# A hybrid decoder layer: its first norm and tail products tile by tile, norm rows loaded early, bias rows late

## What is computed

```
h = rmsnorm(x, norm_mix)
proj = h @ w_in
gate_a, gate_b, z, xbc, dt_raw, c_q, c_kv, kr_raw = jnp.split(proj, SPLIT_POINTS, axis=-1)
ya = ssd_branch(z, xbc, dt_raw, h0, conv_prev, ...)      # causal convolution, chunked scan
yb = mla_branch(c_q, c_kv, kr_raw, ...)                  # latent attention, paged cache
x = x + (sigmoid(gate_a + b) * ya + sigmoid(gate_b + b) * yb) @ w_out
x = x + peer(rmsnorm(x, norm_ffn), ...)                  # 128 gathered experts for each token
```

## Times and profile before

| | us |
|---|---|
| median of 3 runs | 2399.7 |
| lowest and highest of them | 2396.74, 2403.63 |
| the profiled execution, its own time | 2396.4 |
| its span, first to last instruction | 2394.9 |
| PE busy in it | 1992.9 |
| DVE busy | 1516.4 |
| POOL busy | 637.4 |
| ACT busy | 450.7 |

### The profile page before, as it was taken

How to read it: one execution, slowest core, us unless ns; L and a number is a source line. 1 busy time by engine, 2 the same in 40 slices (tenths; PEclk the granted TensorE clock), 3 DMA queues, 4 the chain that set the end, 5 groups by cost and what they waited for, 6 DMA issues and landing times. The chain is left out here.

```text
span 2394.9 us, 26956 instructions
## 1 busy us (share of the span) xinstructions
PE 1992.9 (83%) x9206; PEld 1147.1 (48%) x9206; DVE 1516.4 (63%) x3836; ACT 450.7 (19%) x1358; POOL 637.4 (27%) x592
## 2 busy tenths in 40 slices
PE   6999888898888877777779997878898888777775
PEld 4887655754444422222258875557444443222221
DVE  2464433378777788888524444334787878887874
ACT  1234211121211111111122342101211111111111
POOL 0000000034443444444200000000344434444441
PEclk9999899899999999999979998999999999999998
DMA  5447387399999999999744473873999999999996
GB/s 163 124 142 235 118 294 263 110 375 410 412 416 386 398 388 420 420 420 419 307 150 145 129 250 125 287 254 114 401 414 415 414 386 420 389 420 420 420 418 247
DMA packets 206117, 744.54 MB, mean 311 GB/s; under 512 B 16339, under 2 KB 96651, under 8 KB 137857
## 3 DMA queue, kind: packets, MB, share of 16 engines
q0 software_dynamic: 83008, 581.14, 59.5%
q1 hardware_dynamic: 122960, 161.59, 20.8%
HBM read 731.40 MB, written 11.46 MB: 310 GB/s over the span
## 5 line engine op out<-in xcount | busy, mean ns | idle before, releaser
L1045 PE MATMUL ps<-arena 128*128 128x512 f32 (+1 forms) x2112 | 1012.7, 613 | 234.6 <-DVE arena L1615 234.4
L2117 POOL DMA_INDIRECT arena<-in_peer_uv,arena x528 | 603.4, 1143 | 912.7 <-PE ps L1045 746.6
L1606 DVE CUSTOM_DVE_ANT_0 arena<-arena,h 128x1024 f32<-128x1024 f32 x512 | 627.3, 1225 | 229.1 <-DMA arena<-in_peer_uv,arena 221.6
L1045 PEld LDWEIGHTS ps<-arena 128*128 128x128 f32 (+1 forms) x2112 | 367.8, 188 | 839.3 <-DVE arena L1615 517.8
L484 PE MATMUL ps<-ht_tok,wring 128*128 128x264 f32 (+2 forms) x1728 | 386.3, 380 | 22.8 <-DMA wring<-in_peer_wq 17.1
L484 PEld LDWEIGHTS ps<-ht_tok,wring 128*128 128x128 f32 x1728 | 315.8, 193 | 93.5 <-DMA wring<-in_peer_wq 20.4
L1916 ACT ACTIVATE arena<-arena 128x1 f32<-128x1 f32 x528 | 104.8, 202 | 1027.9 <-DVE arena L1606 1026.6
L1615 DVE TENSOR_SCALAR arena<-consts,arena 128x128 f32<-128x128 f32 (+1 forms) x528 | 181.0, 343 | 30.7 <-ACT arena L1916 30.6
L484 PE MATMUL ps<-arena,wring 128*128 128x264 f32 (+2 forms) x512 | 96.3, 346 | 13.0 <-DMA wring<-in_w_mla_proj 13.0
L484 PEld LDWEIGHTS ps<-arena,wring 128*128 128x128 f32 x512 | 80.9, 200 | 22.9 <-DMA wring<-in_w_mla_proj 13.6
L2101 POOL DMA_DIRECT2D nrow<-in_norm_ffn x2 | 1.1, 534 | 337.8 <-PE ps L802 337.8
(11 more groups left out here) (316 smaller groups left out, 1780.1 us busy)
## 6 DMA issues: line engine op xcount, KB each, us to landing
arena<-in_pages SPq DMA_DIRECT2D x256, 272.0 KB, 4.0
wring<-in_w_in SPq DMA_DIRECT2D x38, 1024.0 KB, 5.7
wring<-in_peer_wq SPq DMA_DIRECT2D x18, 1024.0 KB, 26.1
arena<-in_peer_uv,arena POOLq DMA_INDIRECT x528
h<-in_state_ssm POOLq DMA_DIRECT2D x16, 512.0 KB, 5.3
out<-h POOLq DMA_DIRECT2D x16, 512.0 KB, 4.7
wring<-in_w_ssm_proj SPq DMA_DIRECT2D x8, 1024.0 KB, 8.4
arena<-in_w_out SPq DMA_DIRECT2D x8, 1024.0 KB, 13.2
```

The lines of the kernel that those rows point to most:

```text
L1045: last = pe.matmul(ps[0:outs, SUM_BANK[t] + half, :], diag[:, n % DIAGS, 0:outs], ring[:, HOME[n % RING], D_MODEL + half * 512:D_MODEL + ( ...
L1606: dve.tensor_tensor_reduce(ring[:, HOME[k], 0:D_MODEL], ring[:, HOME[k], 0:D_MODEL], tokens, 1.0, 0.0, ALU.mult, ALU.add, dots[:, column(n ...
L2117: pool.indirect_dma_start(ring[:, HOME[k], :], None, table, bass.IndirectOffsetOnAxis(ap=idx[:, TOPK * u + j:TOPK * u + j + 1], axis=0)).t ...
```

## The change

The reference's arithmetic stays as it is; the order of it and of the loads changes.

- **Norm by tile.** ACT squares tile 0 and takes its root, then squares tiles 1 and 2 and takes both roots. DVE writes `h` tile by tile, with a signal after each. A root of a constant now stands ahead of the squares on ACT.
- **Transposes by tile.** PE turns tile 0 (eight transposes into two banks), then tile 1, then does the first tail product for tile 0, then turns tile 2 (eight small transposes into one bank), then does the tail products of tiles 1 and 2. DVE copies a bank of four chunks at once.
- **Vector rows behind.** The transposes of `vrows` and `cstate` come behind the tail products, and their loads behind weight blocks 0 and 1. ACT's wait for `vt_ready` moves behind the tail.
- **The norm row.** `norm_mix` of both layers and `norm_final` become one tensor `norms`. Row 0 is loaded in the first block. The row of the next layer (or of the final norm) is loaded by POOL in the retrieval, ahead of slot 32. The loads at the start of a layer and of the last block are gone.
- **`wkb` and `wvb`** move on POOL's queue from its start to behind the three states.

```diff
@@ first block, SP
+                sp.dma_start(nrow[:, :], a["norms"][0, :].partition_broadcast(P)).then_inc(sem("first_loads"), 16)
                 sp.wait_ge(sem("x_zeroed"), 1)
@@ PE
+                    def turned_rows(t):
+                        rows = TILES[t][1]
+                        pe.wait_ge(sem("h_ready"), t + 1)
+                        each = 4 if t < 2 else DC
+                        for first in range(0, DC, each):
+                            b = aux.fill()
+                            for c in range(first, first + each):
+                                at = (c - first) * rows
+                                last = turn(ps[:, b, at:at + rows], h[0:rows, t, :].rearrange("p (q c) -> p c q", c=DC)[:, c, :], rows)
+                            aux.filled(last)
+                        marks["ht", t] = aux.n
+                    def first_tail(t):
+                        t0, rows = TILES[t]
+                        pe.wait_ge(sem("aux_free"), 4 + marks["ht", t])
+                        b = wide.fill()
+                        wide.filled(product(ps[0:rows, b, 0:TAIL[0][1]], lambda c: ht[:, c, t0:t0 + rows], lambda c: state["w"][:, c, :], DC))
+                    turned_rows(0)
+                    turned_rows(1)
+                    state["w"] = next_block(DC, TAIL[0][1])
+                    first_tail(0)
+                    turned_rows(2)
+                    marks["ht"] = aux.n
+                    first_tail(1)
+                    first_tail(2)
+                    marks["tail0"] = wide.n
                     pe.wait_ge(sem("vec_loads"), 64)
...
-                    pe.wait_ge(sem("h_ready"), 1)
-                    feature_major(lambda t: h[:, t, :])
-                    marks["ht"] = aux.n
-                    aux.all_emptied()
-                    by_token(*TAIL[0])
-                    marks["tail0"] = wide.n
@@ DVE
+                    rstd(ss[:, 0:1], ss[:, 0:1], rt[:, 0:1], rs[:, 0:1], D_MODEL, "x0_squares", "x0_root")
+                    normed(0)
+                    rstd(ss[:, 1:3], ss[:, 1:3], rt[:, 1:3], rs[:, 1:3], D_MODEL, "x1_squares", "x1_root")
+                    normed(1)
+                    turned_rows(0)
+                    normed(2)
+                    turned_rows(1)
+                    turned_rows(2)
@@ ACT
-                    for t in range(3):
-                        squares(h[:, t, :], x[:, t, :], ss[:, t:t + 1], "x_squares" if t == 2 else None)
-                    root(rt, ss, "x")
-                    act.wait_ge(sem("vt_ready"), 1)
+                    act.activation(st[:, 61:62], ones[:, 0:1], ACT.Sqrt)
+                    squares(h[:, 0, :], x[:, 0, :], ss[:, 0:1], "x0_squares")
+                    root(rt[:, 0:1], ss[:, 0:1], "x0")
+                    squares(h[:, 1, :], x[:, 1, :], ss[:, 1:2])
+                    squares(h[:, 2, :], x[:, 2, :], ss[:, 2:3], "x1_squares")
+                    root(rt[:, 1:3], ss[:, 1:3], "x1")
@@ POOL, retrieval
+                        if n == 2 * TOPK:
+                            pool.wait_ge(sem("ph_ready"), 2)
+                            pool.dma_start(nrow[:, :], of_layer("next_norm", layer).partition_broadcast(P)).then_inc(sem("next_row_load"), 16)
                         pool.indirect_dma_start(ring[:, HOME[k], :], None, table,
```

More of the change, by code:

```diff
@@ L1142, in _, with normed, turned_rows @@
                     then(dve.memset(pad[:, :, 0:PAD], 0.0))
+                    def normed(t):
+                        dve.scalar_tensor_tensor(out=h[:, t, :], in0=x[:, t, :], scalar=rs[:, t:t + 1], in1=nrow[:, :], op0=ALU.mult, op1=ALU.mult).then_inc(sem("h_ready"), 1)
+                    def turned_rows(t):
+                        t0, rows = TILES[t]
+                        each = 4 if t < 2 else DC
+                        for first in range(0, DC, each):
+                            b = aux.read()
+                            aux.emptied(dve.tensor_copy(ht[:, first:first + each, t0:t0 + rows], ps[:, b, 0:each * rows].rearrange("p (c t) -> p c t", c=each)))
+                    rstd(ss[:, 0:1], ss[:, 0:1], rt[:, 0:1], rs[:, 0:1], D_MODEL, "x0_squares", "x0_root")
[6 more added lines that the diff above has]
+                    turned_rows(2)
                     b = aux.read()
@@ L1147, in _ @@
                     dve.nop().then_inc(sem("vt_ready"), 1)
-                    rstd(ss, ss, rt, rs, D_MODEL, "x_squares", "x_root")
-                    dve.wait_ge(sem("nrow_load"), 16)
-                    for t in range(3):
[L1151 to L1154, removed]
                     dve.wait_ge(sem("wide_free"), 4 + marks["tail0"])
@@ L1755, in _ @@
                     act.activation(dtl, dtw, ACT.Ln).then_inc(sem("dt_log"), 1)
+                    act.wait_ge(sem("vt_ready"), 1)
                     pad_out(0)
@@ L1959, in _ @@
                 def _(sp):
[L1961 to L1966, removed]
                     count = [0]
@@ L2011, in _ @@
                     block_of(w_in, XBC, 0)
+                    vr = ssd("vrows")
+                    sp.dma_start(vr[0:CONV * CC, :], of_layer("conv_w", layer).rearrange("k (c p) -> (k c) p", p=P)).then_inc(sem("vec_loads"), 16)
+                    sp.dma_start(vr[CONV * CC:CONV * CC + CC, :], of_layer("conv_b", layer).rearrange("(c p) -> c p", p=P)).then_inc(sem("vec_loads"), 16)
+                    sp.dma_start(vr[V_BIAS:V_NORM, :], of_layer("b_gate", layer).rearrange("(c p) -> c p", p=P)).then_inc(sem("vec_loads"), 16)
+                    sp.dma_start(vr[V_NORM:VEC_ROWS, :], of_layer("ssm_norm", layer).rearrange("(c p) -> c p", p=P)).then_inc(sem("vec_loads"), 16)
                     for v, name in enumerate(("dt_bias", "a_log", "d_skip")):
@@ L2071, in _ @@
                         pool.dma_start(places[b], h0[b]).then_inc(sem(f"state_load{b}"), 16)
+                    pool.dma_start(wkb, of_layer("w_kb", layer)).then_inc(sem("wkv_load"), 16)
+                    pool.dma_start(wvb, of_layer("w_vb", layer)).then_inc(sem("wkv_load"), 16)
                     pool.wait_ge(sem("rawt_ready"), 1)
@@ L2125, in _ @@
                     pool.wait_ge(sem("hs_store"), 16)
-                    for name in ("cstate_load", "wqb_load", "ffn_row_load", "keys_load"):
+                    for name in ("cstate_load", "wqb_load", "ffn_row_load", "keys_load", "next_row_load"):
                         pool.wait_ge(sem(name), 16)
@@ L2174 @@
 _INPUTS = ["x_prompt", "x_sample", "state_ssm", "state_conv", "page_table",
-           "norm_mix", "w_in", "b_gate", "conv_w", "conv_b", "dt_bias", "a_log", "d_skip", "ssm_norm", "w_ssm_proj",
-           "q_norm", "kv_norm", "w_mla_proj", "w_out", "norm_ffn", "peer_wq", "norm_final"]
+           "w_in", "b_gate", "conv_w", "conv_b", "dt_bias", "a_log", "d_skip", "ssm_norm", "w_ssm_proj",
+           "q_norm", "kv_norm", "w_mla_proj", "w_out", "norm_ffn", "peer_wq"]
 _OUTPUTS = [(1, SEQ, D_MODEL), (SAMPLES, 1, D_MODEL), (DEPTH, 1, SEQ, KV_LORA), (DEPTH, 1, SEQ, ROPE),
```

8 lines of the change are left out of this document (3 added, 5 removed).

## The result

The changed kernel takes 2374.36 us (2371.42 to 2376.53, four runs), the kernel before, run beside it, 2398.3: a ratio of 0.990 with a 95% interval of 0.9884 to 0.9916, 23.9 us faster. The profiled execution of the changed kernel took 2376.53, its span is 2375.0.

A forecast was written before the change was run, and what follows sets the result against it. The prediction took the layer heads' serial chain ahead of dense start as the bound. Gains of 9.9 and 8.4 us, less 1.35 and 2 x 1.3, made 14.4 us: 2385.3 from 2399.7, range 2379 to 2392.

The forecast's parts named there:

- What bounds the kernel now: Layer heads: a serial chain leaves PE 22.82 and 21.38 us without products; earlier dense start shortens the layer equally.
- The chain to the second transposes: Layer head, from ACT's first load: transposes of tile 0 begin at 4.62 us, of tile 1 at 7.24.
- The clock within the tail: Tail products in each head: about 5 us at the low clock again, 0.5 us either way.
- the rival in which they raise it: Layer heads: transposes raise the clock before tile 0's products; 5.9 us more, gain 20, time 2379; chance 0.05.
- The vector rows and the state: Behind the tail products: their transposes count in full on PE, 1.80 us, with no wait for loads.
- The price of a transpose: Layer head on PE: a large transpose costs 0.31 us, eight 2.5 us, so the tail starts at 9.75.
- The small ones: Tile 2's eight small transposes in the head count in full on PE: 1.3 us, between 1.0 and 1.6.
- seams: Allowance in each head beside the work moved behind: 0.1 us of the 3.2 us counted there.
- What is paid elsewhere: Outside the heads: 1.35 us for the first-block norm row and 1.3 us twice for rows in the retrievals.
- The row in the retrieval: Next norm row's load in each retrieval: 1.3 us per layer, 0 if hidden, twice that if gathers are upset.
- The retrieval took nothing back: Rival in the retrieval: the row lengthens a PE stall, 3 to 4 us per layer lost; gain 7; chance 0.12.
- the stall for `peer_wq`: Retrieval, 7.39 us on PE; slower rival has it twice more in each, 12.7 us slower, 2412; chance 0.04.

The follow-up runs named there:

- e9: e3 with the eight small sample-tile transposes left out of the first norm's turn, zeros in their place; no total time given, tail products 11.3 us.
- e3: Changed kernel with the old chunk-by-chunk order of transposes, all before the tail products; 2389.4 us, ratio to before 0.9958.
- e1: The changed kernel itself, unaltered, measured again; 2376.2 us against 2400.7 for the kernel before, ratio 0.9906.
- e6: Changed kernel with vector rows' loads, transposes and DVE copies ahead of the norm again; 2388.3 us, ratio to before 0.9958.
- e4: Changed kernel with the next norm row loaded nine times in each retrieval instead of once; 2394.8 us.
- e2: Changed kernel with each large transpose of the layer head done three times into the same place; 2387.3 us in one execution.
- e7: Changed kernel without ACT's root of a constant ahead of the squares; 2379.0 us, ratio to before 0.9911.
- e8: Changed kernel with the next norm row loaded behind the keys, ahead of the retrieval, into its own columns; 2377.2 us, ratio to before 0.9908.

## Why the prediction fell short

**What bounds the kernel now: right.** A microsecond won ahead of dense start is won at the end: 24.5 us in heads and start, 23.9 and 24.5 in the medians.

**The chain to the second transposes: right**, to 0.1 us, in both layers.

**The clock within the tail: wrong, and this is the step that failed.** The prediction said that the transposes ahead "had not raised the clock", expected "the same again", about 5 us at the low level, and gave 0.05 to the rival in which they raise it. The rows of before were read rightly, but taken for a property of transposes. e9 and e3 show that it was the eight small ones among them: with them the clock rose 11.8 us behind the first transpose in layer 1 (13.3 and 12.3 in the two traces of before), without them 2.9. The change collects the small ones behind the first product. That was in the diff, and the prediction priced only their duration. In the changed kernel's first trace the clock rose 5.8 us behind the first transpose in layer 1, 1.5 behind the first product, between forecast and rival; in layer 0 of e1 the rival came true. Which it is in a given head is chance as far as these runs go, and worth up to 1.2 us (3.83 to 5.03 for tile 0). The tail products took 11.8 and 12.2 us for 13.25 and 14.3: 1.4 and 2.1 us. The vector rows and the state, now turned at the high clock, took 1.07 us (1213.42 to 1214.49) for 1.80: 0.7 in each layer. (In e6, where they stand first again, at the low clock, they take 1.80.) So the clock makes some 5 us of the miss in the heads.

**The price of a transpose: mis-sized.** 0.31 us was read off two large ones that had a small one behind them. Eight in a row took 1.97 us, 0.25 each, and from the start of tile 1's to the tail were 1.77: with the earlier `h`, 0.85 us per layer. The small ones took 0.97 us (1204.82 to 1205.79) where 1.3 was taken: 0.3.

These terms make 3.3 us in layer 0 and 4.0 in layer 1, and with the 0.1 taken for seams and the rounding they are the 3.4 and 4.2 by which dense start came ahead of the forecast: 7.6 of the 9.5 to 10 us by which the gain was short.

**What is paid elsewhere: not refuted, with a remainder that stays open.** Layer 0 starts 1.2 us later (9.67 to 10.89, means of two) for 1.35. The row in the retrieval costs 1.16 us by e4, for 1.3. No wait for weight block 0 or the vector rows, none for block 2. By these the changed kernel should pay 3.5 us; start and rest together show 1.6, with a scatter of up to 7 us between executions of one kernel. The 2 us between lie inside it and are not settled. The means of the retrievals in e4 would even put two rows at 3.8 us.

**The rivals.** The retrieval took nothing back that can be told from the row's price; the stall for `peer_wq` is 5.12 and 5.65 us in the changed kernel's first trace, for 7.39 and 5.12 before, and no further one showed. The rule of the Trainium skill on the clock (page "TensorE: Matmul & The Clock Gate", Part 1) was closer than the reading of the rows: large transposes back to back raise the clock as products do, e2 shows it. But it has nothing on small ones among them, for which the rows of before were right. The 2.66 us of the Trainium skill (page "ScalarE: Activation LUTs", What ACT_TABLE_LOAD costs) for a switch of tables did not show in e7. The range was too narrow at the low end, because the clock's turn was given half a microsecond of play per layer, though the rows showed only one order of transposes and the change makes another.

## What to carry to other kernels

A chain of waits at the start of a layer, in which an engine takes up its work in an order that nothing needs, can be forecast to a tenth of a microsecond from single durations. What cannot be carried over is the pace of PE when the change alters what PE does just before: which instructions stand in the stretch in which the clock rises decides some microseconds (e3's heads are 5.4 us longer than e9's). In this kernel it paid to keep the small transposes out of it and to put them behind the first large products. And a load taken off the critical path is worth only what its wait was, less its price in the stage where it lands; here that came to nothing.

## What was not expected of the hardware

- 24 transposes, 16 of 128 rows and 8 of 8 rows in turn, kept PE at the low clock for their 6.7 us and longer; the 16 alone let it rise after 2.9 us in layer 1 of e9. In e2, with 48 large ones, it rose after 5.9 us.
- With one and the same order of instructions the clock rose 3.6 to 6.6 us behind the first transpose in layer 1 (e7; e1 and e8).
- A small transpose of 8 rows between large ones costs more than it does alone: 16 large ones took 3.3 to 3.7 us, with 8 small ones between them 6.7, so 0.4 us each; eight small ones in a row took 0.97 us, 0.12 each.
- The clock column can print 1.00 at the start of an execution while matmuls run at the pace of 0.50, as in layer 0 before; the count of matmuls in a window tells.
- In layer 1 the 1088 KB block of weights took 8.3 us to land with 1.5 MB of other loads ahead and beside it, and 8.3 us without them; in layer 0 9.7 and 7.3 us. In all four a second block of 1 MB follows on its own queue; what part that has in it, no run shows.
